# Value products ahead of the turn in the software-pipelined softmax stages of a two-block mixer kernel

## The reference, cut to what matters

```python
# forgetting attention, one block of 128 queries
logits = einsum('bhqd,bhkd->bhqk', qb, k) * scale + cb[..., None] - cum[:, :, None, :]
out = einsum('bhqk,bhkd->bhqd', softmax(where(causal, logits, -inf)), v)
# differential attention: two softmaxes over 768 keys, one minus lam times the other
a = softmax(einsum('bhcqd,bhckd->bhcqk', q, k) * DIFF_QK ** -0.5)
out = einsum('bhqk,bhkd->bhqd', a[:, :, 0] - lam * a[:, :, 1], v)
# neighbourhood attention: 256 local keys (with a bias) and 256 context keys
a = softmax(concatenate([s_loc, s_ctx]))
out = a_loc @ v_loc + a_ctx @ v_ctx
```

## Time and profile before

| | us |
|---|---|
| median of 3 runs (lowest, highest) | 2161.95 (2155.07, 2167.91) |
| time of the profiled execution | 2166.08 |
| its span in the trace | 2164.3 |
| PE busy | 2092.3 (97%) |
| PEld, DVE, ACT, POOL busy | 1653.5, 1221.1, 729.0, 36.8 |
| mean granted clock of PE | 0.979 of full |

### The profile page before, as it was taken

One profiled execution on the slowest core, in us unless ns is written; L12 is line 12 of the kernel. 1 busy time (PEld: TensorE's weight loads), 2 busy tenths in 40 slices (PEclk: granted clock), 3 DMA queues, 4 the chain that ended last, 5 costly groups with the idle time before them and its releaser, 6 DMA issues.

```text
span 2164.3 us, 30302 instructions
## 1 busy us (share of the span) xinstructions
PE 2092.3 (97%) x11760; PEld 1653.5 (76%) x11760; DVE 1221.1 (56%) x1960; ACT 729.0 (34%) x1169; POOL 36.8 (2%) x69
## 2 busy tenths in 40 slices
PE   6999999999999989999999999999999999999999
PEld 5666765577777777788888888886776786888887
DVE  4763324457446575565666663446466647666644
ACT  4531113644345443321111122334355433222332
POOL 0001000000100000000000000000100000000000
PEclk9999999699999999999999999999999899999999
DMA  5445356432210101112111212121202022222322
GB/s 184 166 156 186 127 177 219 150 98 78 68 49 21 74 1 35 54 59 67 59 60 66 65 62 68 59 68 59 88 30 83 1 69 78 95 91 95 106 91 85
DMA packets 51395, 186.47 MB, mean 86 GB/s; under 512 B 5904, under 2 KB 5904, under 8 KB 50784
## 3 DMA queue, kind: packets, MB, share of 16 engines
q1 hardware_dynamic: 46752, 168.32, 23.3%
q0 software_dynamic: 3168, 13.92, 1.9%
q10 hardware_dynamic: 1376, 2.85, 0.3%
HBM read 181.91 MB, written 3.15 MB: 86 GB/s over the span
## 4 chain that ended last, share of the span: by engine, by line
PE 85%; DVE 7%; ACT 3%; issue 2%; PEld 1%; DMA 0%; ACTq 0%; SPq 0%; PEldq 0%; DVEq 0%
PE psum L229 22%; PE psum L231 21%; PE psum L230 21%; PE psum L730 3%; PE psum L696 3%; PE psum L720 2%; PE psum L1923 2%; PE psum L515 1%; PE psum L2033 1%; PE psum L1427 1%; PE psum L2376 1%; PE psum L708 1%; PE psum L1453 1%; PE psum L518 1%; PE psum L1037 1%
## 5 line engine op out<-in xcount | busy, mean ns | idle before, releaser
L229 PE MATMUL psum<-h_high,unit_high 128*128 128x512 f32 (+1 forms) x1704 | 619.5, 364 | 1.2 <-DVE unit_low L439 1.2
L231 PE MATMUL psum<-h_high,unit_low 128*128 128x512 f32 (+1 forms) x1704 | 609.9, 358 | 0.0
L230 PE MATMUL psum<-h_low,unit_high 128*128 128x512 f32 (+1 forms) x1704 | 608.9, 357 | 0.0
L431 ACT CAST unit_high<-ring 128x1024 fp32r<-128x1024 f32 x194 | 203.2, 1047 | 612.9 <-PE psum L231 603.4
L229 PEld LDWEIGHTS psum<-h_high,unit_high 128*128 128x128 f32 x1704 | 320.3, 188 | 73.0 <-issue 22.6
L439 DVE TENSOR_TENSOR unit_low<-ring,unit_high 128x1024 fp32r<-128x1024 f32 x194 | 236.8, 1221 | 225.8 <-ACT unit_high L431 225.8
L231 PEld LDWEIGHTS psum<-h_high,unit_low 128*128 128x128 f32 x1704 | 320.3, 188 | 48.9
L230 PEld LDWEIGHTS psum<-h_low,unit_high 128*128 128x128 f32 x1704 | 320.3, 188 | 47.8 <-issue 0.7
L2590 DVE TENSOR_SCALAR conv_out<-psum,parameters 128x512 f32<-128x512 f32 (+1 forms) x132 | 91.2, 719 | 174.7 <-PE psum L231 172.4
L2595 DVE SCALAR_TENSOR_TENSOR conv_out<-psum,parameters,conv_out 128x511 f32<-128x511 f32 (+1 forms) x264 | 166.4, 658 | 22.2 <-DVE conv_out L2590 1.5
L801 ACT ACTIVATE probs<-psum,neg_max 128x768 f32<-128x768 f32 (+4 forms) x136 | 98.8, 729 | 148.5 <-DVE neg_max L760 137.5
(11 more groups left out here) (401 smaller groups left out, 2663.0 us busy)
## 6 DMA issues: line engine op xcount, KB each, us to landing
ring<-in_w_units SPq DMA_DIRECT2D x317, 512.0 KB, 3.4
bias<-in_na_bias POOLq DMA_DIRECT2D x2, 1536.0 KB, 9.2
xT<-in_x ACTq DMA_DIRECT2D x4, 512.0 KB, 6.6
xT<-in_x POOLq DMA_DIRECT2D x1, 2048.0 KB, 12.1
dft<-in_dft POOLq DMA_DIRECT2D x2, 1024.0 KB, 5.0
xT<-in_ctx POOLq DMA_DIRECT2D x1, 1024.0 KB, 16.6
rope<-in_rope POOLq DMA_DIRECT2D x2, 512.0 KB, 3.5
v<-na_values POOLq DMA_DIRECT2D x2, 512.0 KB, 4.7
```

Source lines behind the costliest of these rows:

```text
L229: pe.matmul(out, lh, rh, start=first, stop=False, skip_group_check=True)
L230: pe.matmul(out, lh, rl, start=False, stop=False, skip_group_check=True)
L231: return pe.matmul(out, ll, rh, start=False, stop=last, skip_group_check=True)
L431: act.copy(K.w_high[:, q % 2], K.ring[:, q % RING]).then_inc(K.high_split.sem, 1)
```

## The change

In PE's loop of `softmax_attention`, the two last steps of a round change places: mix(t-2) is issued ahead of turn(t-1). Both keep their waits and their instructions. DVE's and ACT's programs are not touched. The loop serves all five softmax stages.

```diff
                 if beside:
                     beside(pe, t)
+                if 0 <= t - 2 < n_items:
+                    mix(t - 2)
                 if 0 <= t - 1 < n_items:
                     turn(t - 1)
-                if 0 <= t - 2 < n_items:
-                    mix(t - 2)
```

## The result

| | before | changed |
|---|---|---|
| median of 20 runs each (lowest, highest), us | 2151.97 (2138.11, 2174.54) | 2160.72 (2143.91, 2182.64) |
| changed to before, 95% interval | | 1.0048 (1.0025 to 1.0070) |
| the same kernels again, 12 runs to 29 | 2151.19 | 2163.40, ratio 1.0063 (1.0029 to 1.0097) |

The change makes the kernel slower by about 0.5%, 9 us (12 us the second time); -2.2 us were forecast. The ratios are taken from the runs in the faster of two states, so that they differ a little from the quotients of the medians. The three runs shown ahead of the prediction (2161.95) lie 10 us above the median of 20, and the profiled one (2166.08) above them. So the old order was profiled once more (span 2138.7 us), and it is that second profile that stands here beside the one of the changed kernel (span 2163.7 us).

The account below looks back on a forecast made before the run. PE, busy for 97% of the span, was taken as the bound. Terms -4.4 - 0.8 - 1.5 + 1.7 + 0.8 + 2.0 = -2.2 us took the median 2161.95 to 2159.8; range 2154 to 2166, whole range 2150 to 2169.

Parts of the forecast that it names:

- The jobs: PE's waits before the sum of squares L2033, 14 times, mostly go as the output step runs under turn: -4.4 us.
- The ends of the differential stages: In the last rounds, mix drawn ahead of turn fills gaps: -1.5 us in layer 1, -0.8 in layer 0.
- The borders: On PE, scores now follow a turn instead of a mix, in 57 rounds: +2.0 us, of 0 to 5.7.
- The wait on the copy: In the neighbourhood stages mix, put first, waits for ACT's copy; with the stages' ends +1.7 us, of 0.8 to 4.
- below 5 us in all: Size forecast for new idle time before mix (L730) that ends on ACT's copy (L809).
- The last item: At the forgetting stage's end, last turn, its copy and last mix follow each other without cover: +0.8 us.
- one rival of 0.08: Copy, mix and turn form a ring and ACT becomes the bound: +26 us, 2186; a new clock fall adds 4 to 6.
- The sign that the prediction named for being wrong: Half clock for longer or shorter stretches than the 14 and 16 us near 754 and 1681.
- The clock does not fall: Filled gaps keep full clock near both differential stages' ends: 2149 for both, chance 0.11; about 2154.5 for one, 0.13.
- The range: The forecast's own 2154 to 2166 us, from its bounds of -9 to +5 and a run scatter of 3 us.
- The reference: Median of the runs shown before the change, 2161.95 us, from which the forecast of 2159.8 was taken.

Follow-up runs that it names:

- kernel 1: Against before, mix goes ahead of turn in the two differential stages alone; ratio 0.9941 (0.9905 to 0.9976).
- kernel 5: Against before, mix ahead of turn in the differential stages only, and there only in rounds that still have scores; ratio 0.9987 (0.9951 to 1.0023).
- kernel 2: Against before, mix goes ahead of turn in the two neighbourhood stages alone; ratio 1.0049 (1.0017 to 1.0082).
- kernel 14: Against before, mix ahead of turn in the neighbourhood stages, and there ACT's sine copy ahead of its copy of the turned probabilities; ratio 1.0019 (0.9983 to 1.0056).
- kernel 18: Against before, order of turn and mix kept, only ACT's sine copy ahead of its turned copy in the neighbourhood stages; ratio 0.9999 (0.9959 to 1.0040).
- kernel 17: Against before, mix ahead of turn only in the last two rounds of the forgetting stage; ratio 1.0043 (1.0004 to 1.0083).
- kernel 3: Against before, mix goes ahead of turn in the forgetting stage alone; ratio 1.0080 (1.0042 to 1.0117).
- kernel 10: Against before, mix of the item three back ahead of turn in the neighbourhood stages, plus the plain swap in the differential stages; ratio 0.9988 (0.9960 to 1.0017).
- kernel 13: Against before, mix ahead of turn in the neighbourhood stages except rounds with a Fourier token transform beside; ratio 1.0051 (1.0014 to 1.0088).

## Why the prediction was wrong

The likeliest case was -2.2 us, within 0.5% of before; measured was +0.5%, the other way. **The step that failed** is that the sum holds the clock fixed: it has no line for new time at half clock, and that is worth +19 us where the rest of the sum is about right. Step by step:

- *The jobs* (-4.4): right, and too small. The 5.3 us ahead of L2033 are 0.3, and the rounds of the differential stages give 7.2 in all. What the other 1.9 and more consist of was not traced; the sum had nothing for the turn's own waits inside the rounds.
- *The ends of the differential stages* (-2.3): 0.8 by kernels 1 and 5. The walk let the last but one copy start at 1670.5 and be over ahead of its mix; in the changed kernel mix waits for a copy twice, 1.55 and 0.89 us:

```profile
1674.19 1.55 PE L730 MATMUL psum<-v,turned 128*128 128x64 f32 x12 [1.55 <-ACT turned L809]
...
1677.29 1.55 PE L730 MATMUL psum<-v,turned 128*128 128x64 f32 x12 [0.89 <-ACT turned L809]
```

- *The borders* (+2.0): nothing, 6.46 us a round in both. The rule weighed there (the Trainium skill, "TensorE: Matmul & The Clock Gate", Part 2) put 0 there, and the trace agrees in the sum, though single borders do differ by 0.10. Turn and mix both have operands of full height, so that the rule prices both orders alike; that borders between two such operands are free does not follow from it as told, and no run tested it.
- *The wait on the copy* (+1.7): 1.2 us of waiting on the copy in layer 0, and 8.7 in all softmax stages ("below 5 us in all" was wrong). It is half of the idle time that the swap adds in layer 0. A second, smaller step that failed is the list of what waits for the delayed turn: "ACT's copy_turned(t-1) and DVE's combine chain wait for these". It stops there. Behind that copy on ACT is the work beside, and in the token rounds DVE and PE wait for it. The one sentence on the queue behind the copy ("nothing ... but mix") looked at a differential round. The two timelines show the wait (2.40 and 3.24 us), and kernels 2, 14 and 18 put its worth in layer 0 at 3.3 of 4.9 us, by one profile each.
- *The last item* (+0.8 in the forgetting stage): as walked: 47.6 (kernel 17) and 48.2 us (kernel 3) against 47.0 in the first profile of before, with the same short fall of the clock. The price left out, if the runs' clocks are read rightly, is the clock behind it.
- *The clock.* The sum held it fixed. The prediction saw that "the copies without cover make new gaps just there" and used it only against a rival, and a new fall had a part in one rival of 0.08. At an equal clock the change is worth about -3 us, near the -2.2 of the sum, though with an error of 3 that is no proof of its terms; 40 us more at half clock are 19 us of time, and turn it into the loss. The sign that the prediction named for being wrong, half clock for longer stretches, is the one that came.
- *"The clock does not fall"* did not pay: kernel 1 has the differential gain at an unchanged time at half clock (59 against 60, 11 either way). It may have come in part, though. The differential stage of layer 1 is at a clock of 1.00 in six of the seven profiles with the whole differential swap, and in five of the thirteen others; in such a profile the saving of 1.2 us that the walk drew from the half clock isn't there to be had.
- *The range.* The bounds of the terms add up to -7 and +10 us, not the "-9 to +5" that was written; the range was drawn too low at its upper end.
- *The reference.* Three runs put before at 2161.95, with 3 us of scatter assumed; 20 runs spread over 36 us, with a median 10 us lower. Against 2162 the changed kernel's 2160.7 would have looked like a hit.

What stays open: why the swap changes the clock, in either kind of stage. Both profiles of the changed kernel have the long stretch from 343 us on, ahead of the forgetting stage's end, which can't be caused by that end. Kernel 17's profile has one behind the stage (0.50 from 391.7 to 425 us), but so have the first profile of before and those of kernels 10 and 14, where the forgetting stage is not swapped. No run separated the two places. The parts at equal clock (-8.7, +2.2, -2.0) sum to -8.5 against -3.4 of the whole, which is at the edge of their error.

## What to carry to other kernels

When a step is moved on one engine, follow every engine's program *behind* each wait on it, in every kind of round, and not only at the stage's end; here a 0.36 us copy that had nothing to do with softmax stood there. On a kernel whose matrix engine changes clock, give the time at half clock a term and a range of its own, read it from every run, and compare kernels at an equal clock before explaining a difference. Apply an order only where it pays: the same swap gave 9 us in one kind of stage and lost 9 to 17 in each of the others.

## What was not expected of the hardware

- With PE busy for 22.62 of 23 and 24.00 of 24 us, the clock stayed at 0.50. Being busy did not bring it back. The Trainium skill ("TensorE: Matmul & The Clock Gate", Part 1) has gaps between bursts send the clock down; the trace agrees behind the gap of 3.24 us in the changed kernel, and kernel 13 fell behind one of 2.40 us that before passes at full clock.
- One and the same program ran its feed-forward at two paces, both at full clock. The kernel before, first profile, then second:

```profile
1132.50:1182.50 50.00, 50.00 (x289) 44.01 (x289) 30.95 (x45) 8.85 (x9) 0.00 (x0) 1.00 0.19 63
```

```profile
1127.30:1177.30 50.00, 50.00 (x297) 44.13 (x296) 30.94 (x45) 8.85 (x9) 0.00 (x0) 1.00 0.20 65
```

289 or 297 matmuls in 50 us; 128x256 matmuls (L229 to L231) follow each other by 0.118 or 0.113 us, those of 128x512 by 0.229 in both. It makes 9.5 us between the layers, as much as the whole effect studied here, and no run tells what sets it.
